# Slot tables from bf16 one-hot products, the slot table written before the weights' parts, and VectorE's order at the first expert

## The chip, the cores and the metric

The kernel runs on one core of a Trainium2 chip. The metric is the device time of one execution in microseconds (us), as the median of several executions. Matrix products run on TensorE (PE), elementwise work on VectorE (DVE) and ScalarE (ACT), gathers and some elementwise work on GpSimd (POOL), and SyncE (SP) issues most DMAs.

## The reference, cut to what matters

One decoder layer: a token mixer (not touched by the change), then a grouped top-2 mixture of 16 experts over 1024 tokens of width 1024.

```python
scores = jax.nn.sigmoid((hf @ w_router).astype(f32))
...                                    # best group of 4, top 2 experts in it: e_idx
w = jnp.take_along_axis(scores, e_idx, axis=-1)
w = w / jnp.sum(w, axis=-1, keepdims=True)
...
slot_tok = jnp.full((n_blk * MOE_BLOCK,), N, jnp.int32).at[dest].set((order // TOP_K).astype(jnp.int32))
slot_w = jnp.zeros((n_blk * MOE_BLOCK,), hf.dtype).at[dest].set(w.reshape(-1)[order].astype(hf.dtype))
...
a = jax.nn.silu(jnp.einsum('nrd,ndf->nrf', xs, w_gate[blk_e])) * jnp.einsum('nrd,ndf->nrf', xs, w_up[blk_e])
y = jnp.einsum('nrf,nfd->nrd', a, w_down[blk_e]).reshape(-1, D) * slot_w[:, None]
out = jnp.zeros((N + 1, D), hf.dtype).at[slot_tok].add(y)[:N]
```

Each (token, choice) pair has a slot in a list sorted by expert. `slot_tok` says which token sits in a slot and `slot_w` with what weight.

## The kernel before

**The stages.** The program runs adaLN rows and projections, then attention, the branch mix and output projection, the router, then routing tables and the experts. Each engine has its own program in order, and semaphores join them. The change lies between the router and the first expert's products, and everything behind it is the expert loop.

**The routing tables.** There are 1024 tokens in 8 tiles of 128, each with two choices, so 16 columns `a` (tile and choice) of 128 partitions. VectorE computes the slot of each pair (`dest`, L1471), splits it into position in the block (`pb_f[:, 0]`) and block number (`pb_f[:, 1]`), and builds one-hot tables: `hot_b` (L1477; 16 x 32 blocks), `hot_t` (L1480; `hot_b` times token number less position less 1024) and `hot_p` (L1483, in two halves of 8 columns; 16 x 128 positions). All are float32. Most of these instructions go through `own`, which makes VectorE wait for each result before the next one.

TensorE then adds up 16 products `hot_p[a]` x `hot_t[a]` in PSUM (L1900), which gives the token of each slot in [128 positions, 32 blocks], and 16 products `hot_p[a]` x `hot_b[a]` (L1904), where `hot_b` has by then been multiplied by the normalised weights (L1492). VectorE turns the first into `slot_idx` (L1495) and copies the second into `slot_w` (L1497).

**What follows.** GpSimd waits for `slot_ok` (L772), copies a column of `slot_idx` (L753) and gathers 128 rows of tokens into `xs` (L756). TensorE turns them (`expert_tokens`, L1911), ScalarE rounds them to a first part `xs_hi` (L998), VectorE makes the rest `xs_lo` (`expert_tokens_lo`, L1509). GpSimd issues the second block's gather and then subtracts the last sixth of the expert's weights (`expert_weights_rest`, L769).

**The weights of an expert** (gate, up, down, each [128, 4096] per partition) are split in the same way: ScalarE makes the first parts in six chunks of 2048 (L994), VectorE the rests of chunks 1 to 5 (`expert_weights_lo`, L1503), GpSimd the sixth. A product then takes three matmuls (L1921, L1922, L1926 for gate and up; L1964, L1965, L1969 for down).

**VectorE's order at the first expert** before: wait for `slot_w_full`, copy `slot_w`, five subtractions of L1503, `expert_tokens_lo(0)`, then, in its sequencer, `wait_ge(slot_w_ok)` and a `nop` that raises `a_ok` (L1526), then `expert_out(0)`. TensorE's first product waits for two things:

```python
pe.wait_ge(xs_lo_ok, j + 1)      # L1941
pe.wait_ge(a_ok, j * 2 + 1)      # L1942
```

Later it waits for the rests of the weights as it comes to them: `w_lo_ok` 1 and 2 in the gate's third pass, 3 and 4 in that of up, 5 and `w_lo_pool` in down.

Of the kernel before, what the change touches and what calls it, by code (L numbers as in the profile page):

```python
# [13 lines left out]
ALU = mybir.AluOpType  # L14
ACT = mybir.ActivationFunctionType
AX = mybir.AxisListType
F32 = mybir.dt.float32
F32R = mybir.dt.float32r
BF16 = mybir.dt.bfloat16
# [3 lines left out]
P = 128  # L23
BANK = 512
# [35 lines left out]
def hybrid_trunk(nc, x, c, w_ada, b_ada, g_norm_mix, g_norm_moe, w_in, cmp_pe_k, cmp_w1_k, cmp_w2_k, cmp_pe_v,  # L60
                 cmp_w1_v, cmp_w2_v, nsa_q_gain, nsa_k_gain, swa_q_gain, swa_k_gain, swa_sinks, w_branch_a,
                 w_branch_b, w_branch_c, w_out, w_router, router_bias, w_exp_gate, w_exp_up, w_exp_down, out):
    _, T, D = x.shape
    NT, NK = T // P, D // P
# [19 lines left out]
    with ctx:  # L84
        def sb(name, shape, dt=F32):
            return ctx.enter_context(nc.sbuf_tensor(name, shape, dt))
# [32 lines left out]
        bc, bc_r = twice("bc", [P, 8 * T])  # L119
# [5 lines left out]
        swa_bias = sb("swa_bias", [P, SWA_H, 2 * P])  # L125
# [13 lines left out]
        psum = ctx.enter_context(nc.psum_tensor("psum", [P, 8, BANK], F32))  # L139
# [76 lines left out]
        for i in ORDER:  # L216
            s = slot_of(i)
# [204 lines left out]
        def z_group(m):  # L422
# [20 lines left out]
        N_BLK = 2 * T // P + NE  # L443
# [18 lines left out]
        w12, dest_f = sb("w12", [P, 2, NT]), sb("dest_f", [P, 2, NT])  # L462
        dest = sb("dest", [P, 2, NT], U32)
        plan_f, plan_i = sb("plan_f", [P, 2 * NE + 2]), sb("plan_i", [P, 2 * NE + 2], I32)
        slot_idx, slot_w = sb("slot_idx", [P, N_BLK + 4], U32), sb("slot_w", [P, N_BLK + 4])
        in_idx, out_idx, w_cur = sb("in_idx", [P, 1], U32), sb("out_idx", [P, 1], U32), sb("w_cur", [P, 1])
        pb_u, pb_f = sb("pb_u", [P, 2, 2 * NT], U32), sb("pb_f", [P, 2, 2 * NT])
        tok_less, spare_row = sb("tok_less", [P, 2 * NT]), sb("spare_row", [P, 1])
        iota_p, iota_b = swa_bias[:, 0, 0:P], swa_bias[:, 1, 0:N_BLK]
        hot_p = bc[:, 6 * D:8 * D].rearrange("p (a s) -> p a s", a=2 * NT)  # L470
        hot_b, hot_t = (bc[:, 4 * D + i * BANK:4 * D + (i + 1) * BANK].rearrange("p (a b) -> p a b", a=2 * NT) for i in range(2))
        score_ok, chosen_ok, rank_full, dest_ok, routing_tables = (sem(s) for s in (
            "score_ok", "chosen_ok", "rank_full", "dest_ok", "routing_tables"))
        hot_ok, hot_w_ok, slot_full, slot_w_full, slot_ok, slot_w_ok = (sem(s) for s in (
            "hot_ok", "hot_w_ok", "slot_full", "slot_w_full", "slot_ok", "slot_w_ok"))
# [142 lines left out]
        def _(pool):  # L618
            one = Chain(pool, pool_own)
# [3 lines left out]
                                   pattern=[[-1, P]], channel_multiplier=1))  # L623
# [44 lines left out]
            for t, base, step, mult in ((tri_causal, 0, -1, 1), (tri_low, -1, 1, -1), (tri_strict, -1, -1, 1)):  # L668
# [3 lines left out]
                                       pattern=[[step, P]], channel_multiplier=mult))  # L672
            one(pool.memset(stair[:, :], 0.0))
            one(pool.affine_select(out=stair[:, :], in_=stair[:, :], compare_op=ALU.is_ge, fill=MASKED,
                                   base=16 * 56 - (CMP_LEN - 1), pattern=[[-CMP_STRIDE, 120]], channel_multiplier=1))

            one(pool.iota(swa_bias[:, 0, :], pattern=[[-1, 2 * P]], base=P, channel_multiplier=1,
                          allow_small_or_imprecise_dtypes=True))
# [8 lines left out]
            for k in (kwinT, kslcT):  # L687
# [3 lines left out]
                                       pattern=[[0, T]], channel_multiplier=1))  # L691
# [3 lines left out]
                                   pattern=[[1, T]], channel_multiplier=-SEL_BLOCK))  # L695
            one(pool.affine_select(out=blocks, in_=blocks, compare_op=ALU.is_ge, fill=0.0, base=SEL_BLOCK - 1,
                                   pattern=[[-1, T]], channel_multiplier=SEL_BLOCK))
            cend = kcmpT[ROW_POS:ROW_SEL, :]
            one(pool.iota(cend, pattern=[[CMP_STRIDE, NC + 1]], base=CMP_LEN - 1, channel_multiplier=0,
                          allow_small_or_imprecise_dtypes=True))  # L700
            one(pool.affine_select(out=cend, in_=cend, compare_op=ALU.is_equal, fill=0.0, base=0,
                                   pattern=[[0, NC + 1]], channel_multiplier=1))

            one(pool.iota(force[:, :, :], pattern=[[-2, NT], [1, NSEL]], base=0, channel_multiplier=0,
                          allow_small_or_imprecise_dtypes=True))
            pool.iota(stp[:, 30:31], pattern=[[0, 1]], base=0, channel_multiplier=1,
                      allow_small_or_imprecise_dtypes=True).then_inc(tables, 1)
# [10 lines left out]
            for m, r in enumerate(rides):  # L718
                w = width(r)
                pool.wait_ge(sb_z, m + 1)  # L720
                if m:
# [4 lines left out]
                          allow_small_or_imprecise_dtypes=True))  # L726
            one(pool.iota(iota_m[:, :], pattern=[[P, NT]], base=0, channel_multiplier=0,
                          allow_small_or_imprecise_dtypes=True))
            one(pool.iota(slot_idx[:, :], pattern=[[0, N_BLK + 4]], base=T, channel_multiplier=1))
            one(pool.memset(slot_w[:, :], 0.0))  # L730
            one(pool.iota(tok_less[:, :].rearrange("p (j n) -> p j n", j=2), pattern=[[0, 2], [P, NT]], base=-T,
                          channel_multiplier=1, allow_small_or_imprecise_dtypes=True))
            one(pool.iota(spare_row[:, :], pattern=[[0, 1]], base=T, channel_multiplier=1,
                          allow_small_or_imprecise_dtypes=True))
            pool.wait_ge(mix_done, 1)
# [5 lines left out]
                               pattern=[[1, P]], channel_multiplier=-1).then_inc(routing_tables, 1)  # L741
# [286 lines left out]
        def _(dve):  # L1028
            own = Chain(dve, dve_own)
# [83 lines left out]
            for s in range(4 * NT + 1):  # L1113
                ch, n = divmod(s, NT)
                a = psum[:, 4 + s % 3, :]
# [149 lines left out]
            for q, s in enumerate(slots):  # L1265
                n, i, u = s["n"], s["i"], s["unit"]
# [74 lines left out]
            for r in range(3 * 2 * NK):  # L1341
                m, b, hf = r // 6, r // 2 % 3, r % 2
# [112 lines left out]
            nb, base, last = plan_f[:, 0:NE], plan_f[:, NE:2 * NE], plan_f[:, 2 * NE:2 * NE + 1]  # L1455
# [12 lines left out]
            for j, oh in enumerate((oh1, oh2)):  # L1468
# [7 lines left out]
            own(dve.tensor_copy(pb_f[:, :, :], pb_u[:, :, :]))  # L1476
            own(dve.tensor_tensor(hot_b, iota_b.unsqueeze(1).to_broadcast([P, 2 * NT, N_BLK]),  # L1477
                                  pb_f[:, 1, :].unsqueeze(2).to_broadcast([P, 2 * NT, N_BLK]), ALU.is_equal))
            own(dve.tensor_tensor(tok_less[:, :], tok_less[:, :], pb_f[:, 0, :], ALU.subtract))
            own(dve.tensor_tensor(hot_t, hot_b, tok_less[:, :].unsqueeze(2).to_broadcast([P, 2 * NT, N_BLK]), ALU.mult))  # L1480
            for i in range(2):
                js = slice(i * NT, (i + 1) * NT)
                dve.tensor_tensor(hot_p[:, js, :], iota_p.unsqueeze(1).to_broadcast([P, NT, P]),  # L1483
# [1 line left out]
            for j, oh in enumerate((oh1, oh2)):  # L1485
                own(dve.tensor_tensor(t_a, score, oh, ALU.mult))
                own(dve.tensor_reduce(w12[:, j, :], t_a, AX.X, ALU.add))
            own(dve.tensor_tensor(red[1], w12[:, 0, :], w12[:, 1, :], ALU.add))
            own(dve.reciprocal(red[1], red[1]))
            for j in range(2):  # L1490
                own(dve.tensor_tensor(w12[:, j, :], w12[:, j, :], red[1], ALU.mult))
            dve.tensor_tensor(hot_b, hot_b, w12[:, :, :].rearrange("p j n -> p (j n)").unsqueeze(2).to_broadcast([P, 2 * NT, N_BLK]),  # L1492
                              ALU.mult).then_inc(hot_w_ok, 1)
            dve.wait_ge(slot_full, 1)
            dve.tensor_scalar(slot_idx[:, 2:N_BLK + 2], psum[:, 6, 0:N_BLK], spare_row[:, 0:1], None, ALU.add).then_inc(slot_ok, 1)  # L1495
            dve.wait_ge(slot_w_full, 1)
            dve.tensor_copy(slot_w[:, 2:N_BLK + 2], psum[:, 4, 0:N_BLK]).then_inc(slot_w_ok, 1)  # L1497

            def expert_weights_lo(e):
                for c in range(5):  # L1500
                    i, cs = c // 2, slice(c % 2 * SLOT // 2, (c % 2 + 1) * SLOT // 2)
                    dve.wait_ge(w_hi_ok, 6 * e + c + 1)
                    dve.tensor_tensor(ew_lo(e, i)[:, cs], w_raw(e, i)[:, cs], ew_hi[i][:, cs].bitcast(F32),  # L1503
                                      ALU.subtract).then_inc(w_lo_ok, 1)

            def expert_tokens_lo(j):
                for h in range(2):
                    dve.wait_ge(xs_hi_ok, j * 2 + h + 1)
                    ins = dve.tensor_tensor(xs_lo[:, 4 * h:4 * h + 4, :], psum[:, 2 + h, :].rearrange("p (k t) -> p k t", k=4),  # L1509
                                            xs_hi[:, 4 * h:4 * h + 4, :].bitcast(F32), ALU.subtract)  # L1510
                ins.then_inc(xs_lo_ok, 1)
# [6 lines left out]
                dve.scalar_tensor_tensor(y_sb.rearrange("p (a d) -> p a d", a=2), psum[:, 5:7, :], w_cur[:, 0:1],  # L1518
                                         gm_bc[:, :].rearrange("p (a d) -> p a d", a=2), ALU.mult, ALU.mult).then_inc(y_scaled, 1)

            expert_weights_lo(0)
            expert_tokens_lo(0)
            dve.wait_ge(dest_ok, 1)
            n_blk = dve.value_load(plan_i[0:1, 2 * NE:2 * NE + 1], min_val=NE, max_val=N_BLK - 1)
            dve.wait_ge(slot_w_ok, 1)
# [24 lines left out]
        def _(pe):  # L1550
# [59 lines left out]
            for s in range(4 * NT + 1):  # L1610
                ch, n = divmod(s, NT)
                if s < 4 * NT:
# [9 lines left out]
                    for k in range(NK):  # L1622
                        mm = pe.matmul(psum[:, 4 + s % 3, 0:w], hT[:, k, n * P:(n + 1) * P],  # L1623
                                       slot(slot_of(L_TOK + ch))[:, k, 0:w], start=(k == 0), stop=(k == NK - 1))
# [31 lines left out]
            for l in range(CMP_LEN):  # L1656
                w = slot(slot_of(L_W1 + l // 16), k=16)
                for a in range(2):
                    rs = slice(a * HD, (a + 1) * HD)
                    mm = pe.matmul(psum[0:NC, a, 0:CMP_HID], blk[rs, l, 0:NC], w[rs, l % 16, :],  # L1660
                                   start=(l == 0), stop=(l == CMP_LEN - 1))
# [10 lines left out]
            for hc in range(2):  # L1672
                pe.matmul(psum[0:64, 2, 0:HD], tmp_gk[:, hc, :], w2[:, 0, hc, :],
                          start=(hc == 0), stop=(hc == 1))
            for hc in range(2):
                mm = pe.matmul(psum[:, 3, 0:HD], tmp_gv[:, hc, :], w2[:, 1, hc, :], start=(hc == 0), stop=(hc == 1))
# [148 lines left out]
            for r in range(3 * 2 * NK):  # L1825
                m, b, hf = r // 6, r // 2 % 3, r % 2
# [14 lines left out]
                for k in range(k0, k1):  # L1841
                    mm = pe.matmul(bank, branch_lo(m)[:, k, :], o_hi[:, ns, k, :], start=False, stop=(k == k1 - 1))
# [9 lines left out]
            for i, m in enumerate((mod_a2, mod_b2)):  # L1852
                for k in range(NK):
                    mm = pe.matmul(psum[:, 4 + 2 * i + k // 4, (k % 4) * P:(k % 4 + 1) * P], m[:, k:k + 1].to_broadcast([P, P]),
                                   ident[:, :], start=True, stop=True)
            mm.then_inc(mod_rows, 1)
            pe.wait_ge(wr_in, 32)
            for n in range(NT + 2):
                if n < NT:
# [11 lines left out]
                    for h in range(2):  # L1871
                        w = wout_lo[h].rearrange("p (k n) -> p k n", k=NK)
                        for k in range(NK):
                            if n == 0 and k % 4 == 0:
                                pe.wait_ge(wout_lo_ok, 2 * h + k // 4 + 1)
                            mm = pe.matmul(psum[:, 2 * (n % 2) + h, :], y_hi[n % 2][:, k, :], w[:, k, :], start=False,
                                           stop=(k == NK - 1))
# [19 lines left out]
            for a in range(2 * NT):  # L1897
                if a % NT == 0:
                    pe.wait_ge(hot_ok, a // NT + 1)
                mm = pe.matmul(psum[:, 6, 0:N_BLK], hot_p[:, a, :], hot_t[:, a, :], start=(a == 0), stop=(a == 2 * NT - 1))  # L1900
            mm.then_inc(slot_full, 1)
            pe.wait_ge(hot_w_ok, 1)
            for a in range(2 * NT):
                mm = pe.matmul(psum[:, 4, 0:N_BLK], hot_p[:, a, :], hot_b[:, a, :], start=(a == 0), stop=(a == 2 * NT - 1))  # L1904
            mm.then_inc(slot_w_full, 1)


# [80 lines left out]
```

## Time and profile before

| | before |
|---|---|
| median of 3 runs | 2009.48 us (2003.45 to 2012.72) |
| the profiled execution's own time | 2009.4 us |
| its span, first to last instruction | 2007.7 us |
| mean granted TensorE clock | 0.947 |
| busy: PE, DVE, ACT, POOL | 91%, 46%, 33%, 18% |
| instructions | 22379 |

The span is 1.7 us less than that execution's own time. Busy shares are averages over all stages. The stage of this change lies in slice 31 of the page's 40, from 1505.8 to 1556.0 us, where PE is busy for three tenths only.

### The profile page before, as it was taken

To read this page: it belongs to the slowest core of one execution; us is meant where nothing else is said; L and a number is where in the kernel's file an instruction comes from. 1 tells how busy PE (TensorE), PEld (TensorE's weight loads), DVE (VectorE), ACT (ScalarE), POOL (GpSimd) and SP (SyncE) were. 2 spreads that over 40 slices of the span, in tenths; PEclk is the share of its full clock that TensorE was granted. 3 is DMA by queue.
4 is the path that set the end of the run, shared out by engine and by line. 5 is a ranking of instruction groups with operands and counts; after the bars stand their busy time and mean duration, and the time that the engine had idled before them with its cause. 6 is when DMAs were issued, how large, how long until landed. Compare 5 with 4: busy or idle time off the path is not lost. (4 is left out here: it accounts for less than half of the span.)

```text
span 2007.7 us, 22379 instructions
## 1 busy us (share of the span) xinstructions
PE 1817.4 (91%) x8125; PEld 1254.0 (62%) x8125; DVE 933.4 (46%) x1517; ACT 664.2 (33%) x1151; POOL 364.3 (18%) x315
## 2 busy tenths in 40 slices
PE   1999999989898989989989978899983999999996
PEld 1555654555555555655656656687873888888885
DVE  5554313232333342434333436477547464648475
ACT  1421101223232333423324325434212353537373
POOL 3211140000010100101102001100001243436344
PEclk9999998999999999999989988799995999999998
DMA  9334321201110010110000010174334586979694
GB/s 340 137 126 147 85 42 34 63 30 40 37 42 26 22 37 27 29 30 22 27 21 23 15 32 1 63 265 175 126 129 164 168 298 205 305 223 381 202 360 131
DMA packets 121395, 232.38 MB, mean 116 GB/s; under 512 B 5832, under 2 KB 44816, under 8 KB 120240
## 3 DMA queue, kind: packets, MB, share of 16 engines
q1 hardware_dynamic: 113312, 203.14, 29.0%
q0 software_dynamic: 7984, 27.93, 5.7%
q8 instruction: 61, 1.00, 0.2%
q14 instruction: 38, 0.31, 0.0%
HBM read 196.97 MB, written 35.13 MB: 116 GB/s over the span
## 5 line engine op out<-in xcount | busy, mean ns | idle before, releaser
L1797 PE MATMUL psum<-arena 128*128 128x512 f32 x768 | 386.7, 639 | 0.5 <-ACT arena L937 0.4
L1279 DVE TENSOR_REDUCE negm<-psum 128x1 f32<-128x640 f32 (+7 forms) x128 | 90.5, 707 | 423.2 <-PE psum L1724 423.2
L1783 PE MATMUL psum<-kv,arena 128*128 128x64 f32 x1464 | 201.6, 283 | 61.9 <-DVE arena L1255 36.7
L1783 PEld LDWEIGHTS psum<-kv,arena 128*128 128x128 f32 x1464 | 192.1, 204 | 69.6 <-issue 38.2
L723 POOL TENSOR_SCALAR arena<-arena 128x128 f32<-128x128 f32 (+7 forms) x32 | 76.8, 2401 | 854.9 <-ACT arena L931 854.9
L1797 PEld LDWEIGHTS psum<-arena 128*128 128x128 f32 x768 | 144.6, 204 | 128.0 <-issue 127.7
L908 ACT ACTIVATE arena<-psum,negm 128x640 f32<-128x640 f32 (+7 forms) x128 | 89.6, 700 | 402.1 <-DVE negm L1279 402.0
L1623 PE MATMUL psum<-arena 128*128 128x512 f32 (+2 forms) x512 | 189.0, 522 | 0.0
L1921 PE MATMUL psum<-heads_r,kv_r 128*128 128x512 f32 x384 | 150.7, 393 | 15.2 <-DVE kv_r L1509 15.2
L1722 PE MATMUL psum<-kv,heads 112*128 112x512 f32 (+7 forms) x384 | 150.7, 498 | 9.2 <-ACT arena L931 8.6
L1503 DVE TENSOR_TENSOR arena_r<-arena,heads_r 128x2048 fp32r<-128x2048 f32 x64 | 146.6, 2353 | 15.1 <-ACT heads_r L994 15.1
L1922 PE MATMUL psum<-heads_r,kv_r 128*128 128x512 f32 x384 | 150.5, 392 | 0.0
L1623 PEld LDWEIGHTS psum<-arena 128*128 128x128 f32 x512 | 95.9, 192 | 76.8 <-issue 73.9
L1751 PE MATMUL psum<-ident,arena 128*128 128x128 f32 x828 | 132.9, 283 | 9.8 <-ACT arena L390 6.1
L1722 PEld LDWEIGHTS psum<-kv,heads 112*128 112x128 f32 (+1 forms) x384 | 74.0, 204 | 95.2 <-issue 85.1
L769 POOL TENSOR_TENSOR arena_r<-arena,bc_r 128x2048 fp32r<-128x2048 f32 x16 | 102.8, 6427 | 107.1 <-ACT bc_r L994 107.0
L1751 PEld LDWEIGHTS psum<-ident,arena 128*128 128x128 f32 x828 | 94.0, 148 | 41.2 <-issue 27.7
L994 ACT ACTIVATE heads_r<-arena 128x2048 fp32r<-128x2048 f32 x64 | 117.3, 1914 | 0.9 <-DMA arena<-in_w_exp_up_dram 0.9
L1926 PE MATMUL psum<-arena_r,kv_r 128*128 128x512 f32 x384 | 95.0, 389 | 0.0
L1921 PEld LDWEIGHTS psum<-heads_r,kv_r 128*128 128x128 f32 x384 | 72.9, 190 | 30.8 <-issue 15.6
L1922 PEld LDWEIGHTS psum<-heads_r,kv_r 128*128 128x128 f32 x384 | 72.8, 190 | 15.2
L1926 PEld LDWEIGHTS psum<-arena_r,kv_r 128*128 128x128 f32 x384 | 72.1, 188 | 15.0
(376 smaller groups left out, 2729.1 us busy)
## 6 DMA issues: line engine op xcount, KB each, us to landing
arena<-in_w_exp_gate_dram SPq DMA_DIRECT2D x16, 2048.0 KB, 12.0
arena<-in_w_exp_down_dram SPq DMA_DIRECT2D x16, 2048.0 KB, 12.5
arena<-in_w_exp_up_dram SPq DMA_DIRECT2D x16, 2048.0 KB, 14.1
arena<-in_w_ada_dram SPq DMA_DIRECT2D x7, 2048.0 KB, 15.6
arena<-in_w_in_dram SPq DMA_DIRECT2D x24, 512.0 KB, 4.0
z_dram<-arena SPq DMA_DIRECT2D x48, 256.0 KB, 2.0
arena<-z_dram SPq DMA_DIRECT2D x8, 1536.0 KB, 7.9
bc<-in_w_ada_dram SPq DMA_DIRECT2D x4, 2048.0 KB, 7.8
```

Source lines behind the costliest of these rows:

```text
L769: pool.tensor_tensor(ew_lo(e, 2)[:, SLOT // 2:SLOT], w_raw(e, 2)[:, SLOT // 2:SLOT], ew_hi[2][:, SLOT // 2:SLOT].bitcast(F32), ALU.subtrac ...
L994: act.activation(ew_hi[i][:, cs], w_raw(e, i)[:, cs], ACT.Copy).then_inc(w_hi_ok, 1)
L1279: dve.tensor_reduce(m1, score_buf(u)[:, 0:w], AX.X, ALU.max, negate=True).then_inc(max_ok, 1)
L1503: dve.tensor_tensor(ew_lo(e, i)[:, cs], w_raw(e, i)[:, cs], ew_hi[i][:, cs].bitcast(F32), ALU.subtract).then_inc(w_lo_ok, 1)
L1623: mm = pe.matmul(psum[:, 4 + s % 3, 0:w], hT[:, k, n * P:(n + 1) * P], slot(slot_of(L_TOK + ch))[:, k, 0:w], start=(k == 0), stop=(k == NK ...
L1722: mm = pe.matmul(b[:, c0:c1], lhs, keys[:, k0 + c0:k0 + c1], start=True, stop=not masks)
L1751: ins = pe.transpose(bank[:, c * P:(c + 1) * P], src[:, t * P:(t + 1) * P], ident[:, :])
L1783: mm = pe.matmul(psum[:, bank, c * HD:(c + 1) * HD], pt[:, j * P:(j + 1) * P], v, start=(j == 0), stop=(j == u["nb"] - 1))
L1797: mm = pe.matmul(GATE_BANK, gate_w[t % 3][:, k, :], hT[:, k, hf * BANK:(hf + 1) * BANK], start=(k == 0), stop=(k == NK - 1))
L1921: pe.matmul(out, xs_hi[:, k, :], w_hi[:, k, :], start=(k == 0), stop=False)
L1922: pe.matmul(out, xs_lo[:, k, :], w_hi[:, k, :], start=False, stop=False)
L1926: mm = pe.matmul(out, xs_hi[:, k, :], w_lo[:, k, :], start=False, stop=(k == NK - 1))
```

## The change

The one-hot tables become bf16, and values that bf16 can't hold in one piece are split. The token of a slot is the sum of two products (`tile_row`, a multiple of 128, and `tok_rest`, partition less position), the weight the sum of three (`w_part`, three bf16 parts). The parts sit side by side in the columns of one matmul: 64 columns for the tokens, 96 for the weights. VectorE writes `slot_idx` before it computes the weights' parts. At the first expert it now does three subtractions of L1503, then `slot_w` (a reduction over the three parts in PSUM), then `expert_tokens_lo(0)`, then the other two subtractions.

```diff
+        hot_p = bc[:, 6 * D:7 * D].bitcast(BF16).rearrange("p (a s) -> p a s", a=2 * NT)
+        hot_b = bc[:, 4 * D:4 * D + 256].bitcast(BF16).rearrange("p (a b) -> p a b", a=2 * NT)
+        hot_t = bc[:, 4 * D + 256:4 * D + 768].bitcast(BF16).rearrange("p (a c b) -> p a c b", a=2 * NT, c=2)
+        hot_w = bc[:, 7 * D:7 * D + 768].bitcast(BF16).rearrange("p (a c b) -> p a c b", a=2 * NT, c=3)
...
-            one(pool.iota(tok_less[:, :].rearrange("p (j n) -> p j n", j=2), pattern=[[0, 2], [P, NT]], base=-T,
-                          channel_multiplier=1, allow_small_or_imprecise_dtypes=True))
+            one(pool.iota(tile_row[:, :].rearrange("p (j n) -> p j n", j=2), pattern=[[0, 2], [P, NT]], base=-T,
+                          channel_multiplier=0, allow_small_or_imprecise_dtypes=True))
+            one(pool.iota(tok_rest[:, :], pattern=[[0, 2 * NT]], base=0, channel_multiplier=1, allow_small_or_imprecise_dtypes=True))
...
-            own(dve.tensor_tensor(tok_less[:, :], tok_less[:, :], pb_f[:, 0, :], ALU.subtract))
-            own(dve.tensor_tensor(hot_t, hot_b, tok_less[:, :].unsqueeze(2).to_broadcast([P, 2 * NT, N_BLK]), ALU.mult))
+            own(dve.tensor_tensor(tok_rest[:, :], tok_rest[:, :], pb_f[:, 0, :], ALU.subtract))
+            for c, v in enumerate((tile_row, tok_rest)):
+                own(dve.tensor_tensor(hot_t[:, :, c, :], hot_b, v[:, :].unsqueeze(2).to_broadcast([P, 2 * NT, N_BLK]), ALU.mult))
...
+            dve.wait_ge(slot_full, 1)
+            own(dve.tensor_scalar(slot_part, psum[:, 6, 0:N_BLK], spare_row[:, 0:1], None, ALU.add))
+            dve.tensor_tensor(slot_idx[:, 2:N_BLK + 2], slot_part, psum[:, 6, N_BLK:2 * N_BLK], ALU.add).then_inc(slot_ok, 1)
             own(dve.tensor_tensor(red[1], w12[:, 0, :], w12[:, 1, :], ALU.add))
             own(dve.reciprocal(red[1], red[1]))
             for j in range(2):
                 own(dve.tensor_tensor(w12[:, j, :], w12[:, j, :], red[1], ALU.mult))
-            dve.tensor_tensor(hot_b, hot_b, w12[:, :, :].rearrange("p j n -> p (j n)").unsqueeze(2).to_broadcast([P, 2 * NT, N_BLK]),
-                              ALU.mult).then_inc(hot_w_ok, 1)
-            dve.wait_ge(slot_full, 1)
-            dve.tensor_scalar(slot_idx[:, 2:N_BLK + 2], psum[:, 6, 0:N_BLK], spare_row[:, 0:1], None, ALU.add).then_inc(slot_ok, 1)
-            dve.wait_ge(slot_w_full, 1)
-            dve.tensor_copy(slot_w[:, 2:N_BLK + 2], psum[:, 4, 0:N_BLK]).then_inc(slot_w_ok, 1)
-
-            def expert_weights_lo(e):
-                for c in range(5):
+            w16 = w12[:, :, :].rearrange("p j n -> p (j n)")
+            own(dve.tensor_copy(w_part[:, :, 0], w16))
+            own(dve.tensor_tensor(w_left[:, :], w16, w_part[:, :, 0], ALU.subtract))
+            own(dve.tensor_copy(w_part[:, :, 1], w_left[:, :]))
+            own(dve.tensor_tensor(w_left[:, :], w_left[:, :], w_part[:, :, 1], ALU.subtract))
+            own(dve.tensor_copy(w_part[:, :, 2], w_left[:, :]))
+            dve.tensor_tensor(hot_w, hot_b.unsqueeze(2).to_broadcast([P, 2 * NT, 3, N_BLK]),
+                              w_part[:, :, :].unsqueeze(3).to_broadcast([P, 2 * NT, 3, N_BLK]), ALU.mult).then_inc(hot_w_ok, 1)
+
+            def expert_weights_lo(e, chunks=range(5)):
+                for c in chunks:
...
-            expert_weights_lo(0)
+            expert_weights_lo(0, range(3))
+            dve.wait_ge(slot_w_full, 1)
+            dve.tensor_reduce(slot_w[:, 2:N_BLK + 2], psum[:, 4, 0:3 * N_BLK].rearrange("p (c b) -> p b c", c=3), AX.X,
+                              ALU.add).then_inc(slot_w_ok, 1)
             expert_tokens_lo(0)
+            expert_weights_lo(0, range(3, 5))
...
-                mm = pe.matmul(psum[:, 6, 0:N_BLK], hot_p[:, a, :], hot_t[:, a, :], start=(a == 0), stop=(a == 2 * NT - 1))
+                mm = pe.matmul(psum[:, 6, 0:2 * N_BLK], hot_p[:, a, :], hot_t[:, a, :, :].rearrange("p c b -> p (c b)"),
+                               start=(a == 0), stop=(a == 2 * NT - 1))
...
-                mm = pe.matmul(psum[:, 4, 0:N_BLK], hot_p[:, a, :], hot_b[:, a, :], start=(a == 0), stop=(a == 2 * NT - 1))
+                mm = pe.matmul(psum[:, 4, 0:3 * N_BLK], hot_p[:, a, :], hot_w[:, a, :, :].rearrange("p c b -> p (c b)"),
+                               start=(a == 0), stop=(a == 2 * NT - 1))
```

## Rows read from the trace of the kernel before

**Rows 1.** Windows: busy us of each engine (instructions), granted PE clock, DMA share, GB/s.

```profile
1522.90:1529.70 6.80, 6.79 (x32) 6.79 (x33) 3.55 (x10) 0.00 (x0) 0.00 (x0) 0.50 0.18 73
...
1538.60:1553.70 15.10, 0.00 (x0) 0.00 (x0) 15.06 (x9) 2.35 (x3) 8.44 (x3) 0.50 0.12 35
1553.70:1557.90 4.20, 4.14 (x10) 3.30 (x11) 1.19 (x1) 0.00 (x0) 1.84 (x2) 0.50 0.00 0
...
1800.00:1900.00 100.00, 99.54 (x467) 81.42 (x467) 67.97 (x67) 56.58 (x53) 48.59 (x26) 1.00 0.89 303
```

**Rows 2.** Waits from 1553.7 us to the end: engine, releaser, total us, times, longest.

```profile
PE psum L1921 <- DVE kv_r L1509: 15.2, 1, 15.2
```

**Rows 3.** Chain that ended last, 1536 to 1554 us: start, us, what.

```profile
1540.63 0.02 DVEq L1526
...
1543.53 8.78 DVE arena_r L1503 x2
1552.31 1.21 DVE kv_r L1509 x2
...
1553.76 0.76 PE psum L1921
```

**Rows 4.** Timeline from the one-hot tables on: start, us, engine, line [idle before].

```profile
1519.98 0.69 DVE L1477 TENSOR_TENSOR bc<-swa_bias,pb_f 128x512 f32<-128x512 f32 x1
...
1521.64 2.36 DVE L1483 TENSOR_TENSOR bc<-swa_bias,pb_f 128x1024 f32<-128x1024 f32 x2
...
1522.91 7.04 PE L1900 MATMUL psum<-bc 128*128 128x32 f32 x32 [10.25 <-DVE bc L1483]
...
1525.20 0.17 DVE L1488 TENSOR_TENSOR kv<-w 128x8 f32<-128x8 f32 x1
...
1526.04 0.69 DVE L1492 TENSOR_TENSOR bc<-bc,w 128x512 f32<-128x512 f32 x1
...
1529.77 7.01 PE L1904 MATMUL psum<-bc 128*128 128x32 f32 x32
1529.99 0.25 DVE L1495 TENSOR_SCALAR slot_idx<-psum,spare_row 128x32 uint32<-128x32 f32 x1 [3.27 <-PE psum L1900]
...
1536.59 1.95 PE L1911 MATMUL psum<-ident,kv 128*128 128x128 f32 x8
1536.82 0.19 DVE L1497 COPY slot_w<-psum 128x32 f32<-128x32 f32 x1 [6.57 <-PE psum L1904]
...
1538.58 1.08 ACT L998 ACTIVATE kv_r<-psum 128x512 fp32r<-128x512 f32 x2 [22.30 <-PE psum L1911]
```

**Rows 5.** Timeline, DVE, 1547 to 1549 us.

```profile
1543.53 6.58 DVE L1503 TENSOR_TENSOR arena_r<-arena,heads_r 128x2048 fp32r<-128x2048 f32 x1
```

**Rows 6.** Timeline, POOL, the first two gathers and its share of the weights.

```profile
1531.50 1.12 POOL L756 DMA_INDIRECT kv<-xn_dram,in_idx  x1 [0.89 <-POOL in_idx L753]
1538.69 0.56 POOL L753 COPY in_idx<-slot_idx 128x1 uint32<-128x1 uint32 x1 [6.07 <-PE psum L1911]
1540.05 2.21 POOL L756 DMA_INDIRECT kv<-xn_dram,in_idx  x1 [0.81 <-POOL in_idx L753]
1542.30 5.67 POOL L769 TENSOR_TENSOR arena_r<-arena,bc_r 128x2048 fp32r<-128x2048 f32 x1
```

**Rows 7.** Timeline at the second expert, DVE, then POOL.

```profile
1598.55 2.29 DVE L1503 TENSOR_TENSOR arena_r<-arena,bc_r 128x2048 fp32r<-128x2048 f32 x1
...
1600.94 1.28 DVE L1518 SCALAR_TENSOR_TENSOR bc<-psum,w_cur,gm_bc 128x1024 f32<-128x1024 f32 x1
...
1598.81 6.49 POOL L769 TENSOR_TENSOR arena_r<-arena,bc_r 128x2048 fp32r<-128x2048 f32 x1 [9.87 <-ACT bc_r L994]
```

**Rows 8.** Instructions of the bf16 product at L1895.

```profile
L1895 PEld LDWEIGHTS psum<-chosen,before_b x1: 106/106/106, 1512.3 to 1512.3; 128*128 128x128 bf16 x1
L1895 PE MATMUL psum<-chosen,before_b x1: 266/266/266, 1512.3 to 1512.3; 128*128 128x128 bf16 x1
```

**Rows 9.** Gathers into `kv`, first two, issue to landing.

```profile
DMA to landing us min/median/max: 4.3/4.9/5.5
```

More of the change, by code:

```diff
@@ L467, in hybrid_trunk @@
         pb_u, pb_f = sb("pb_u", [P, 2, 2 * NT], U32), sb("pb_f", [P, 2, 2 * NT])
-        tok_less, spare_row = sb("tok_less", [P, 2 * NT]), sb("spare_row", [P, 1])
+        tile_row, tok_rest, spare_row = sb("tile_row", [P, 2 * NT]), sb("tok_rest", [P, 2 * NT]), sb("spare_row", [P, 1])
+        w_part, w_left = sb("w_part", [P, 2 * NT, 3], BF16), sb("w_left", [P, 2 * NT])
         iota_p, iota_b = swa_bias[:, 0, 0:P], swa_bias[:, 1, 0:N_BLK]
-        hot_p = bc[:, 6 * D:8 * D].rearrange("p (a s) -> p a s", a=2 * NT)
-        hot_b, hot_t = (bc[:, 4 * D + i * BANK:4 * D + (i + 1) * BANK].rearrange("p (a b) -> p a b", a=2 * NT) for i in range(2))
+        slot_part = swa_bias[:, 2, 0:N_BLK]
+        hot_p = bc[:, 6 * D:7 * D].bitcast(BF16).rearrange("p (a s) -> p a s", a=2 * NT)
+        hot_b = bc[:, 4 * D:4 * D + 256].bitcast(BF16).rearrange("p (a b) -> p a b", a=2 * NT)
+        hot_t = bc[:, 4 * D + 256:4 * D + 768].bitcast(BF16).rearrange("p (a c b) -> p a c b", a=2 * NT, c=2)
+        hot_w = bc[:, 7 * D:7 * D + 768].bitcast(BF16).rearrange("p (a c b) -> p a c b", a=2 * NT, c=3)
         score_ok, chosen_ok, rank_full, dest_ok, routing_tables = (sem(s) for s in (
```

## The prediction

> **What bounds the kernel now.** I read the windows first. In the expert loop, shown from 1800 to 1900 us, PE is busy for over 99% of the time at the full clock, and in the stretch of the change it stands still: 15.1 us without one product [rows 1]. The waits from the first expert's product to the end hold one row of PE as a waiting engine, the 15.2 us in front of that product [rows 2]. So what is won ahead of it should reach the end one for one: the next experts' weights, gathers and adds all wait for events of the loop and move with it. The question is when L1921 starts, now at 1553.76.
>
> The chain of waits [rows 3] and the timeline [rows 4] tell how that time comes about. One-hot tables until 1524.00; 16 products for the token table, 7.04 us; 16 for the weights, 7.01 us; the rows turned and `slot_w` copied until 1537.01. Then VectorE alone: five subtractions, then `expert_tokens_lo`, which runs from 1552.31 to 1553.52, and PE starts 0.24 later. Between 1537.01 and 1552.31 lie 15.30 us for five instructions. The last of the five follows the fourth after its 6.58 us and ends in 8.78 us with it, so one takes 2.20, five take 11.0, and 4.3 are a stall of the fourth [rows 3, 5].
>
> The stall is GpSimd's. Its own subtraction runs from 1542.30 to 1547.97, and the VectorE instruction that starts at 1543.53 ends 2.1 us behind that, about its normal length [rows 5, 6]. At the second expert the order is reversed: VectorE's subtraction ends at 1600.84, and GpSimd's, begun at 1598.81, ends at 1605.30, 4.46 us later [rows 7]. The two engines take turns on such instructions. But L1518, which reads PSUM and SBUF, runs at 1600.94 in its plain 1.28 us under that same GpSimd instruction [rows 7].
>
> **Tables and token products.** The second `hot_t` product costs VectorE one more 512-element instruction, 0.69 plus 0.04 of hand-over: 0.73 (two of these and a small one took 1521.64 - 1519.98 = 1.66 [rows 4]). `hot_p` ends at 1524.00 + 0.73 = 1524.73. The output type alone should not change VectorE's pace here, as inputs stay float32. The first eight products hide behind the second half of `hot_p`; the other eight follow it. A bf16 load of 128x128 takes 0.106 us and the product behind it 0.266, most of it latency [rows 8]. Overlapped they cost some 0.11 each, so 0.9 plus 0.3 for the last: slot_full at 1526.0, where it was 1529.99 [rows 4]. Bounds: not overlapped at all, 8 x 0.37 = 3.0, so 1527.8; if the loads cost half, 1525.6. I take 0.11, since in the float32 products, too, the pitch is near one load (7.04 / 32 = 0.22).
>
> VectorE reaches that wait at 1525.20 + 0.73 = 1525.93, so it is hardly early. Two instructions like L1495 (0.25 each, 0.04 between) write `slot_idx` at 1526.54, where it was 1530.24: 3.7 us earlier [rows 4].
>
> **Weights' parts.** Normalising takes 1526.04 - 1525.20 = 0.84, four instructions of 0.21. Five more such small ones: 1.05. `hot_w` has 1536 elements: between 1.18 for 1024 and 2.29 for 2048, so 1.73 [rows 4, 7]. VectorE is free at 1526.54 + 0.84 + 1.05 + 1.73 = 1530.16. Bound above: a four-dimensional pattern at half pace, 3.4; below: two elements at a time, the time of 768, between 0.69 for 512 and 1.18 for 1024, 0.94. The Trainium skill (VectorE: DVE Perf Modes, Mode 2×_1P) has 16-bit operands in steps of one run at two per cycle; `w_part` is broadcast with step 0, so by that rule too it would be the slow way. Were it the quick one, PE would start 0.8 us earlier still. No row here has such an instruction.
>
> **The weight products leave the path.** They run from 1530.2: 16 x 0.11 + 0.2 is 2.0 us, to 1532.2 (5.9 if not overlapped: 1536.1), while VectorE already subtracts. Their cover is 6.6 us of subtractions, up to 1536.8.
>
> **Gather.** From the end of L1495 to the gather's issue are 1531.50 - 1530.24 = 1.26 us, and 4.3 to its landing [rows 4, 6, 9]: 1526.54 + 5.56 = 1532.1. PE then turns the rows from 1532.2, ScalarE comes 2.0 us behind its start (1538.58 against 1536.59) and takes 1.08: `xs_hi` is done by 1535.4 [rows 4]. If PE's unoverlapped end of 1536.1 held, this would be 1539.2.
>
> **The reordered piece.** Three subtractions, 6.6: 1536.8. The reduction of `slot_w`, a PSUM read of 96 elements, 0.3 (L1495 took 0.25 for 32): 1537.1. `expert_tokens_lo` 1.21: 1538.3. PE 0.24 later: 1538.55. That is 15.2 us sooner than 1553.76. By terms: VectorE's first subtraction starts at 1530.16, not 1537.01 (6.85); two subtractions go behind (4.4); the stall goes behind (4.3); the reduction replaces nothing in that span (-0.3); sum 15.2.
>
> **Where the stall goes.** GpSimd's second gather starts when the rows are turned, near 1534.5, and its subtraction came 3.6 us after that (1542.30 - 1538.69 [rows 6]): 1538.1, or up to 2.3 later. That is behind the third subtraction in any case, and `expert_tokens_lo` reads PSUM, like L1518, so the stall falls on the fourth or fifth: VectorE ends them at 1538.3 + 4.4 + 4.4 = 1547.1. PE needs the fourth's result only at its 44th product (24 of gate, 16 of up's first passes, 4 of the third); at the loop's full-clock mean of 99.54 / 467 = 0.21 us [rows 1] that is at least 9.4 us in, 1547.9, and the fourth is done by 1544.9 even with the whole stall on it. The fifth comes after 48 products and the transposes, over 10.2 us in, 1548.8 or later, against 1547.1. The cover is 3 and 1.7 us at the least. What is late next is VectorE itself: `xs_lo` waits for its three subtractions, not for the rows.
>
> **The condition on it.** PE also waits for `a_ok`, and the `nop` that raises it stands behind all five subtractions. Before, the same `nop` went out at 1540.63, while the second of five was being computed: VectorE's sequencer runs ahead of its engine, with the rest queued [rows 3]. It needs `slot_w_ok` (1537.1 now), so it should fire near 1537.2, ahead of `xs_lo`.
>
> **Rivals.**
> *A. The sequencer does not run ahead, so PE waits for all five subtractions.* Then 1547.1 + 0.3 = 1547.4, a gain of 6.4: 2003.0 us. Against it stands the row at 1540.63; for it, that the queue now also holds the reduction. 8 in 100.
> *B. GpSimd's turn comes before the third subtraction.* It would add 4.4: a gain of 10.8, 1998.6 us. For that its second gather would have to be through by 1534.6, when it has only just begun. 6 in 100.
> *C. The first gather is held up by VectorE,* which was idle at 1530 to 1537 and is now busy. The copy of 0.56 and the issue of 2.21 us, against 1.12 for the first, show what that costs when long subtractions run: 1.5 us [rows 6]; twice a whole instruction would be 4.5. The rows then come at 1536.6, `xs_hi` at 1539.9, `xs_lo` 0.6 later; PE near 1540.8: a gain of 13, 1996.4 us. 8 in 100. The Trainium skill (GPSIMD Engine Reference, Key points) says that GpSimd contends with VectorE instructions that have two SBUF inputs, which `hot_w` and the subtractions are; by that, the gather's index copy could wait for one of them. The rows agree in kind.
> *D, the other side: the low clock holds on.* PE was busy for 6.79 of 6.80 us with the float32 table products, and its clock stayed at 0.50, 1.2 GHz; the loop's first 4.2 us, ten products, ran at 0.50 too, and those from 1800 on at 1.00 [rows 1]. Each further us at half clock costs about half a us: a clock that stays low for 30 us more eats the gain, for 50 us more makes it slower by 0.5%. The loop's products are the same as before and follow each other as before, so 3 in 100. A start a few us earlier or later against the clock's rise is worth 1 to 2 us either way.
> *E. Something outside cancels it,* such as a loop that is held by weight transfers (DMA share 0.89 between 1800 and 1900 [rows 1]), so that less than 5 us arrives: 5 in 100. Against it: PE is busy 99.54 of 100 us there, and the transfers are started by PE's own steps.
>
> **How the numbers follow.** The likeliest, at 70 in 100: 15.2 us off the profiled execution's 2009.4 (span 2007.7 plus 1.7 around it; the median of the three runs is 2009.48, the same): 1994.2 us. Its own range is 1989 to 1999: the three runs differ by 9 us, so their median may be off by 3; bounds of `hot_w` (+0.8, -1.7), products (+0.4, -1.8), clock (2). Eight in ten over all cases: 1988.5 to 2003, which takes in A, B and C. Within 0.5%, 10 us, is about what a measurement of this kernel can't tell from no change. Faster by more (below 1999.4): nearly all of the likeliest (0.66), C (0.07) and half of B (0.03), so 0.76. Within: the rest of these, A, E, so 0.21. Slower: 0.03 from D.
>
> **What would show it.** L1921 first starts at 1538 to 1539; before it VectorE shows three subtractions of 2.28 without a gap from about 1530, a reduction, two L1509s; the nop near 1537. The instruction of 6.6 us is the fourth or fifth subtraction, behind PE's start. L1904 takes some 2 us and hides. If L1921 still follows the fifth subtraction, A holds; if one of the first three is 6.6 long, B. The prediction is wrong if PE then waits in the first block for `w_lo_ok`, or if the loop's length from L1921 to the end is no longer 454 us.

## The result, and the profile after

| | before | after |
|---|---|---|
| median | 2004.98 us (2003.45 to 2012.72, 5 runs) | 1991.39 us (1989.98 to 1996.44, 5 runs) |
| ratio, 95% interval | 1 | 0.9930 (0.9913 to 0.9946) |
| profiled execution, span | 2009.4, 2007.7 us | 1993.5, 1991.7 us |

The kernel is faster by 0.7%, 14 us at the ratio. Forecast were 1994.2 us and 15.2 us of gain. The next fences show how the 16.0 us between the two spans come about.

The chain of waits of the changed kernel from 1534 us on; L1514 is the weights' subtraction (L1503 before), L1520 `expert_tokens_lo`, L1938 the first expert product (L1921 before); "DVEq" is VectorE's sequencer, and it answers to [rows 3]:

```profile
1536.43 0.22 DVEq L1539
...
1537.00 0.25 DVE slot_w L1534
...
1537.39 0.32 DVEq L1544
...
1537.93 0.53 DVE kv_r L1520
1538.46 0.24 issue
1538.70 0.77 PE psum L1938
```

The first product starts at 1538.70 where it was 1553.76, 0.24 us behind `xs_lo`. At 1536.43 the sequencer is at L1539, code that stands behind all five subtractions, while the third is being computed (until 1537.09). It has gone ahead, as at 1540.63 before, and passes the `nop` (L1541, an event semaphore in the trace) at 1537.3, ahead of the end of `xs_lo`:

```profile
L1541 DVEq EVENT_SEMAPHORE  x1: 21/21/21, 1537.3 to 1537.3; - x1
```

The timeline of VectorE (L1482 is `hot_b`, L1486 the two `hot_t`, L1489 `hot_p`), against [rows 4, 5]:

```profile
1520.48 0.69 DVE L1482 TENSOR_TENSOR bc<-swa_bias,pb_f 128x512 bf16<-128x512 f32 x1
...
1522.14 0.69 DVE L1486 TENSOR_TENSOR bc<-bc,tok_rest 128x512 bf16<-128x512 bf16 x1
1522.87 2.36 DVE L1489 TENSOR_TENSOR bc<-swa_bias,pb_f 128x1024 bf16<-128x1024 f32 x2
...
1526.43 0.25 DVE L1495 TENSOR_SCALAR swa_bias<-psum,spare_row 128x32 f32<-128x32 f32 x1
1526.72 0.19 DVE L1496 TENSOR_TENSOR slot_idx<-swa_bias,psum 128x32 uint32<-128x32 f32 x1
...
1528.72 1.76 DVE L1507 TENSOR_TENSOR bc<-bc,w_part 128x1536 bf16<-128x1536 bf16 x1
1530.40 6.69 DVE L1514 TENSOR_TENSOR arena_r<-arena,heads_r 128x2048 fp32r<-128x2048 f32 x3
1537.00 0.25 DVE L1534 TENSOR_REDUCE slot_w<-psum 128x32 f32<-128x96 f32 x1
1537.17 1.28 DVE L1520 TENSOR_TENSOR kv_r<-psum,kv_r 128x512 fp32r<-128x512 f32 x2
1538.37 2.28 DVE L1514 TENSOR_TENSOR arena_r<-arena,heads_r 128x2048 fp32r<-128x2048 f32 x1
1540.57 6.68 DVE L1514 TENSOR_TENSOR arena_r<-arena,bc_r 128x2048 fp32r<-128x2048 f32 x1
```

From `hot_b` to the first product are now 1538.70 - 1520.48 = 18.22 us, where they were 1553.76 - 1519.98 = 33.78: 15.56 less. This stage length is the measure in all that follows. The instruction with the stall, 6.68 us, is the fifth subtraction, and it starts 1.9 us behind PE.

PE's timeline of the table products (L1915 tokens, L1920 weights) and of the rows' turning:

```profile
1524.15 0.61 PE L1915 MATMUL psum<-bc 128*128 128x64 bf16 x8 [10.98 <-DVE bc L1489]
1525.29 0.61 PE L1915 MATMUL psum<-bc 128*128 128x64 bf16 x8 [0.53 <-DVE bc L1489]
1530.54 1.46 PE L1920 MATMUL psum<-bc 128*128 128x96 bf16 x16 [4.64 <-DVE bc L1507]
1532.71 1.97 PE L1928 MATMUL psum<-ident,kv 128*128 128x128 f32 x8 [0.71 <-DMA kv<-xn_dram,in_idx]
```

14 us of float32 products have become 2.7. The weights' products end at 1532.0, inside the first subtraction, and PE then waits 0.71 for the gather.

GpSimd's timeline, against [rows 6] (L758 the index copy, L761 the gather, L774 its subtraction):

```profile
1528.16 1.12 POOL L761 DMA_INDIRECT kv<-xn_dram,in_idx  x1 [0.89 <-POOL in_idx L758]
1534.82 2.31 POOL L758 COPY in_idx<-slot_idx 128x1 uint32<-128x1 uint32 x1 [5.55 <-PE psum L1928]
1537.94 0.99 POOL L761 DMA_INDIRECT kv<-xn_dram,in_idx  x1 [0.81 <-POOL in_idx L758]
1538.95 6.15 POOL L774 TENSOR_TENSOR arena_r<-arena,bc_r 128x2048 fp32r<-128x2048 f32 x1
```

The first gather's issue took 1.12 us, as before. It began while VectorE had only short instructions. `hot_w`, which has two inputs in SBUF, began 0.56 us later, at 1528.72, and didn't lengthen it. In the same way the second issue took 0.99 us, though a subtraction began 0.43 us into it. The second index copy ends at 1537.13, right behind VectorE's third subtraction (1537.09).

Windows of the first products, against [rows 1]:

```profile
1538.70:1541.60 2.90, 2.90 (x7) 2.32 (x8) 2.90 (x2) 0.00 (x0) 2.87 (x2) 0.51 0.55 174
1541.70:1545.00 3.30, 3.30 (x16) 2.71 (x15) 3.30 (x1) 0.00 (x0) 3.30 (x1) 1.00 0.02 9
```

PE's clock reached 2.4 GHz after seven products and 2.9 us, not after ten and some 4.2. From the first product to the end of the span are 453.0 us, 0.9 less than the 453.9 before; in the eleven profiles of this document that length lies between 452.6 and 454.5, so the 0.9 can't be put down to the change. Together: stage -15.6, loop -0.9, and `hot_b` itself started 0.5 later, so -16.0.

### The profile page after: what moved, and what is told of

It is laid out like the page before. It is cut to its first block and busy times, and to the rows that moved or that the text cites. A ratio compares the mean times of both kernels' runs of the same rounds, so it can differ in the third digit from the quotient of the medians.

```text
span 1991.7 us, 22324 instructions
## 1 busy us (share of the span) xinstructions
PE 1805.6 (91%) x8093; PEld 1241.9 (62%) x8093; DVE 936.9 (47%) x1524; ACT 664.2 (33%) x1151; POOL 365.6 (18%) x316
## 5 line engine op out<-in xcount | busy, mean ns | idle before, releaser
L1938 PE MATMUL psum<-heads_r,kv_r 128*128 128x512 f32 x384 | 150.3, 391 | 4.0 <-DVE kv_r L1520 4.0
L1514 DVE TENSOR_TENSOR arena_r<-arena,heads_r 128x2048 fp32r<-128x2048 f32 x64 | 142.5, 2286 | 15.1 <-ACT heads_r L999 15.1
L774 POOL TENSOR_TENSOR arena_r<-arena,bc_r 128x2048 fp32r<-128x2048 f32 x16 | 103.4, 6464 | 106.9 <-ACT bc_r L999 106.9
L1938 PEld LDWEIGHTS psum<-heads_r,kv_r 128*128 128x128 f32 x384 | 72.6, 189 | 19.5 <-issue 4.4
```

The lines of the kernel that those rows point to most:

```text
L774: pool.tensor_tensor(ew_lo(e, 2)[:, SLOT // 2:SLOT], w_raw(e, 2)[:, SLOT // 2:SLOT], ew_hi[2][:, SLOT // 2:SLOT].bitcast(F32), ALU.subtrac ...
L1938: pe.matmul(out, xs_hi[:, k, :], w_hi[:, k, :], start=(k == 0), stop=False)
```

## The experiments

Each kernel was timed beside the kernel before. "Stage" is the time from `hot_b` to the first expert product in its profile.

| kernel | stage us | less than before | ratio to the kernel before (95%) |
|---|---|---|---|
| before | 33.78 | | 1 |
| after | 18.22 | 15.6 | 0.9930 (0.9913 to 0.9946) |
| after again | 18.21 | 15.6 | 0.9929 (0.9916 to 0.9941) |
| old order, new tables | 28.56 | 5.2 | 0.9971 (0.9958 to 0.9985) |
| new order, old tables | 23.15 | 10.6 | 0.9952 (0.9934 to 0.9969) |
| `a_ok` held | 26.46 | 7.3 | 0.9959 (0.9945 to 0.9973) |
| before, no GpSimd share | 29.48 | 4.3 | 0.9976 (0.9958 to 0.9993) |
| `slot_idx` late | 22.81 | 11.0 | 0.9962 (0.9949 to 0.9975) |
| new order, old tables, after the copy | 21.50 | 12.3 | 0.9940 (0.9921 to 0.9959) |
| two first | 16.28 | 17.5 | 0.9913 (0.9899 to 0.9927) |
| two first, `slot_idx` sooner | 16.22 | 17.6 | 0.9927 (0.9913 to 0.9942) |

**The tables with the old order.** The edit to the changed kernel:

```diff
-            expert_weights_lo(0, range(3))
             dve.wait_ge(slot_w_full, 1)
             dve.tensor_reduce(slot_w[:, 2:N_BLK + 2], ...).then_inc(slot_w_ok, 1)
+            expert_weights_lo(0)
             expert_tokens_lo(0)
-            expert_weights_lo(0, range(3, 5))
```

> The changed kernel with VectorE's old order at the first expert (wait for the weight products, write slot_w, five subtractions, then xs_lo). Measured as the time from the start of hot_b to the first expert product: 33.8 us before, 18.2 us after. My theory, order and tables both count: the subtractions start when the bf16 weight products are through, some 2 us later than after, and two subtractions (4.4) and GpSimd's turn (4.3) come back in front of PE: 28.6 us, about 5 us under the kernel before. Rival, the tables bring the gain and the order is free: near 20 us and 13 us under the kernel before. Rival, the tables bring nothing: 33 us.

The stage took 28.56 us. VectorE's timeline in it:

```profile
1527.54 0.26 DVE L1533 TENSOR_REDUCE slot_w<-psum 128x32 f32<-128x96 f32 x1 [1.56 <-PE psum L1919]
1527.71 8.89 DVE L1514 TENSOR_TENSOR arena_r<-arena,heads_r 128x2048 fp32r<-128x2048 f32 x4
1536.52 6.58 DVE L1514 TENSOR_TENSOR arena_r<-arena,bc_r 128x2048 fp32r<-128x2048 f32 x1
1543.03 1.28 DVE L1520 TENSOR_TENSOR kv_r<-psum,kv_r 128x512 fp32r<-128x512 f32 x2
```

VectorE waits 1.56 us for the weights' products, and the 6.58 us stall is back ahead of `xs_lo`. The tables alone bring 5.2 us. With them in place, the order is worth the other 10.3.

**The order with the old tables.** The edit to the kernel before:

```diff
-            dve.wait_ge(slot_w_full, 1)
-            dve.tensor_copy(slot_w[:, 2:N_BLK + 2], psum[:, 4, 0:N_BLK]).then_inc(slot_w_ok, 1)
...
-            expert_weights_lo(0)
+            expert_weights_lo(0, range(3))
+            dve.wait_ge(slot_w_full, 1)
+            dve.tensor_copy(slot_w[:, 2:N_BLK + 2], psum[:, 4, 0:N_BLK]).then_inc(slot_w_ok, 1)
             expert_tokens_lo(0)
+            expert_weights_lo(0, range(3, 5))
```

> The kernel before, float32 tables, with only the new order (three subtractions, slot_w, xs_lo, two subtractions). My theory: VectorE is free at once after slot_idx, so its three subtractions hide the float32 weight products, and what is late is the gather, whose index copy now meets a subtraction and waits some 2 us for it. Rows near 1538, turned, split: 22.1 us from hot_b to the first product, 11 to 12 us under the kernel before. Rival, the two engines don't meet on so small a copy: 20 to 21 us, PE bound by its own float32 products. Rival, the order is worth only the two subtractions and the stall behind it (8.7): 25 us.

It took 23.15 us, 1.0 more than my number, and the timelines of GpSimd and of PE say where:

```profile
1524.81 2.07 POOL L753 COPY in_idx<-slot_idx 128x1 uint32<-128x1 uint32 x1 [35.29 <-DVE slot_idx L1495]
1527.77 2.25 POOL L756 DMA_INDIRECT kv<-xn_dram,in_idx  x1 [0.89 <-POOL in_idx L753]
```

```profile
1524.16 7.01 PE L1905 MATMUL psum<-bc 128*128 128x32 f32 x32
1533.35 1.97 PE L1912 MATMUL psum<-ident,kv 128*128 128x128 f32 x8 [2.18 <-DMA kv<-xn_dram,in_idx]
```

I had counted one meeting, that is, one wait of GpSimd for a VectorE subtraction to end. There were two: the index copy took 2.07 us instead of 0.18, and the issue 2.25 instead of 1.12. PE was through with its float32 products and waited 2.18 us for the rows. So the order alone gives 10.6 of the 15.6 us, and the bf16 tables add 4.9 on top.

**Is it a meeting?** The same kernel with one line ahead of the first subtraction:

```diff
+            dve.wait_ge(in_idx_ok, 1)
             expert_weights_lo(0, range(3))
```

> The kernel with float32 tables and the new order alone (23.1 us from hot_b to the first product), and one wait more: VectorE begins its first subtraction only when GpSimd has copied the gather's index. In the run without that wait the index copy took 2.07 us and the gather's issue 2.25, against 0.18 and 1.12 in the kernel before. My theory: each of the two meets one subtraction. With the wait the copy takes 0.18 again, the issue still meets a subtraction and stays near 2.2, the rows land 1.9 us sooner, and PE starts at 21.2 us, although VectorE starts 0.4 later. Rival: the copy is slow for another reason, such as GpSimd waking from a long wait: copy and 23.1 stay, or become 23.5. Rival: the bound is PE's float32 products: 22 to 23.

```profile
1523.67 0.18 POOL L753 COPY in_idx<-slot_idx 128x1 uint32<-128x1 uint32 x1 [35.28 <-DVE slot_idx L1495]
1524.75 2.42 POOL L756 DMA_INDIRECT kv<-xn_dram,in_idx  x1 [0.89 <-POOL in_idx L753]
```

The copy is back to 0.18, the issue, which no wait protects, took 2.42, and the stage is 1.65 us shorter (21.50, where 21.2 was expected), though VectorE waited 0.40 us for the copy. The rows came 0.5 us behind the last float32 product, so the rival with PE as the bound is out as well. The Trainium skill (GPSIMD Engine Reference, Key points) names two SBUF inputs on VectorE as what contends with GpSimd. The copy agrees with it, and so does L1518 of [rows 7], which reads PSUM and ran at its plain length beside GpSimd's subtraction. The runs show the turns and their lengths, not what the two engines share.

**`slot_idx` late.** In the changed kernel the three lines from `wait_ge(slot_full, 1)` to `slot_ok` were moved behind `hot_w`.

> The changed kernel with slot_idx written behind hot_w, as the kernel before did. slot_idx comes 3.7 us later, straight ahead of the first subtraction. My theory: GpSimd's index copy then meets that subtraction and waits for it (2.1 us), so that the rows land at 1538.0 and PE starts 21.6 us after hot_b, 3.4 later than after the change. Without that meeting the rows land at 1536 and PE starts at 19.7. If the place of slot_idx doesn't matter because VectorE is the bound: 18.2.

```profile
1528.69 2.07 POOL L758 COPY in_idx<-slot_idx 128x1 uint32<-128x1 uint32 x1 [35.01 <-DVE slot_idx L1508]
1531.65 2.25 POOL L761 DMA_INDIRECT kv<-xn_dram,in_idx  x1 [0.89 <-POOL in_idx L758]
```

It took 22.81 us, 4.6 more than after and 1.2 more than expected, for the same reason: copy 2.07 and issue 2.25, two meetings. PE stood 7.51 us in front of the rows. The rows' turning began 18.6 us behind `hot_b`, not 12.2: 3.6 come from the later write and 3.0 from the two meetings (1.9 and 1.1), 0.2 more than the 6.4 together, and 4.6 reached PE. That is what the move of `slot_idx` in the change is worth with the rest in place. The timing agrees only loosely here (0.9962, 7.6 us, where the stage says 11.0; the interval reaches to 10.2).

**What the running ahead is worth.** In the changed kernel, before the `nop` that raises `a_ok`:

```diff
             dve.wait_ge(slot_w_ok, 1)
+            dve.wait_ge(w_lo_ok, 5)
             dve.nop().then_inc(a_ok, 1)
```

> The changed kernel, where VectorE's sequencer waits for all five subtractions before the nop that raises a_ok. It shows what rival A would have cost. PE's first product then follows the fifth subtraction: 27.0 us from hot_b instead of 18.2, 8.8 us slower than the changed kernel. If the sequencer's running ahead were not what let PE go, nothing would change: 18.2.

```profile
1544.47 0.80 PE L1939 MATMUL psum<-heads_r,kv_r 128*128 128x512 f32 x1 [12.34 <-DVEq L1542]
```

PE waited 12.34 us, now for the sequencer. The stage took 26.46 us, 8.2 more than after and 0.5 less than expected. Had the sequencer not gone ahead, more than half of the gain would have been lost.

**Whose stall it was.** In the kernel before, GpSimd's subtraction was left out at the first expert and VectorE did it behind `expert_tokens_lo`:

```diff
-                expert_weights_rest(e)
+                if e:
+                    expert_weights_rest(e)
...
             expert_tokens_lo(0)
+            dve.wait_ge(w_hi_ok, 6)
+            dve.tensor_tensor(ew_lo(0, 2)[:, SLOT // 2:SLOT], w_raw(0, 2)[:, SLOT // 2:SLOT], ew_hi[2][:, SLOT // 2:SLOT].bitcast(F32),
+                              ALU.subtract).then_inc(w_lo_pool, 1)
```

> The kernel before, with GpSimd's subtraction left out at the first expert and done by VectorE behind xs_lo. If the 4.3 us in the fourth subtraction are GpSimd's turn, all five take 2.28 and the first product comes 4.3 us sooner: 29.5 us from hot_b instead of 33.8. If they are something else on VectorE (a weight transfer, code loading), a subtraction of 6.6 us stays and so does 33.8.

```profile
1535.02 8.89 DVE L1504 TENSOR_TENSOR arena_r<-arena,heads_r 128x2048 fp32r<-128x2048 f32 x4
1543.82 2.28 DVE L1504 TENSOR_TENSOR arena_r<-arena,bc_r 128x2048 fp32r<-128x2048 f32 x1
```

All five subtractions now have their plain length, and the stage is 4.3 us shorter. The 4.3 us were GpSimd's turn.

**A better split.** After the change the rows were split by 1535.8 us while VectorE's third subtraction ran until 1537.1. So two ahead of `slot_w` and `xs_lo`, three behind; the changed kernel ran once more with it.

> The changed kernel once more, as the mate of the next three on one chip: 18.2 us from hot_b to the first product, 0.993 of the kernel before.

```diff
-            expert_weights_lo(0, range(3))
+            expert_weights_lo(0, range(2))
...
-            expert_weights_lo(0, range(3, 5))
+            expert_weights_lo(0, range(2, 5))
```

> The changed kernel with two subtractions ahead of slot_w and xs_lo instead of three. After the change the rows are split by ScalarE at 1535.8 while VectorE is busy with its third subtraction until 1537.0. My theory: with two, PE starts when the gather's path ends, 16.3 us from hot_b instead of 18.2, and the three late subtractions with GpSimd's turn still lie under PE's first products: about 2 us faster than the changed kernel, no wait of PE for w_lo_ok. Rival: the third one, or GpSimd's turn in front of it, comes too late for PE, which then waits in up's third pass: no gain. Rival: the path is VectorE's in another way and 18.2 stays.

The chain of waits in it:

```profile
1529.44 0.61 ACT kv_r L1003
...
1530.07 0.69 DVE kv_r L1520
...
1531.49 0.03 DVEq L1541
1531.53 0.08 issue
1531.61 0.77 PE psum L1938
```

The stage took 16.28 us, 1.9 less than after, and the chain now comes from ScalarE's split of the rows. PE never waited for `w_lo_ok`. The profile names the `nop` at 1531.49 as its release, 0.13 us behind the end of `xs_lo`, since the sequencer comes to that code only when it has passed the wait for `xs_hi`. But PE starts 0.25 us behind `xs_lo`, where the kernel before has 0.24, so the `nop` delays nothing that can be measured; whether it would bind on a still shorter path is not shown. The medians of that session were 1987.88 us for this kernel and 1991.62 for the changed one. Each of its four runs was faster than each of the five of the changed kernel, but the two intervals in the table overlap, so the gain over the change is shown by the stage and only made likely by the times.

**And `slot_idx` sooner.** As the last one, with the wait for `slot_full` and the two instructions behind it placed after the first half (`j == 0`) of the loop at L1491 of the changed kernel.

> As the one before, and slot_idx written after the first half of the gathering of the weights, not after both. After the change slot_full came at 1525.9, but VectorE took it up at 1526.4. If the gather's path bounds the start, this moves it by another 0.5 us: 15.8 us from hot_b. If not, 16.3 as in the one before.

A miss: 16.22 us, not 15.8. `slot_idx` was 0.4 us sooner, but `expert_tokens_lo` no longer waited for ScalarE. It followed the reduction, at 1530.17, 14.7 us behind `hot_b` as before, because VectorE had the same work ahead of it and now waited 0.25 us for `slot_full`. The bound had gone back to VectorE. The times say 14.6 us for this kernel where the stage says 17.6, and the interval (11.6 to 17.5) just misses it; its six runs fall between 1987.5 and 1995.1 us.

## Why the prediction was right

Numbers are us behind `hot_b`, forecast (from 1519.98) and measured (from 1520.48).

- **Tables.** `hot_p` done at 4.75, measured 4.75. One more `hot_t` instruction was its whole price.
- **Token products.** slot_full at 6.0, measured 5.4. The term was mis-sized: eight products took 0.61 us with the last, not 1.2. It changed little, since VectorE came to that wait at 5.95, as forecast. `slot_idx` was ready at 6.43 against 6.56: 0.07 from the wait, 0.06 from its second instruction, which took 0.19 and not 0.25. The ground for 0.11 us a product was also misread: the float32 pitch of 0.22 is not near one load, whose record is 0.33 us:

```profile
L1900 PEld LDWEIGHTS psum<-bc x32: 288/333/338, 1522.9 to 1529.5; 128*128 128x128 f32 x32
```

- **Weights' parts.** 10.18, measured 10.00. `hot_w` took 1.76 us (forecast 1.73), so it kept the pace of the float32 rows, though both inputs are bf16. The rule of the Trainium skill for 16-bit operands (VectorE: DVE Perf Modes, Mode 2×_1P) asks for steps of one, and the step of 0 fits with the slow pace.
- **Gather.** Rows in at 12.1, measured 12.2. Rival C didn't come about: copy and issue of the first gather began among short instructions. The experiments show that it was a real danger: with a subtraction right behind `slot_idx` the rows come some 3 us later by two meetings, between the 1.5 and the 4.5 of the prediction.
- **Reordered piece.** First product at 18.57, measured 18.22.
- **The stall** went behind PE's start, on the fifth subtraction, and nobody waited for it. Rival B fails with it.
- **The condition on `a_ok`** held (rival A, measured at 26.46 us of stage, a gain of 7.3 where I had put 6.4).
- **The clock** rose sooner, not later (rival D), and the loop passed on all of the gain (rival E): from the first product to the end 453.0 us against 453.9, as good as the same.

The forecast of 15.2 us stood against 15.6 in the stage and 15.9 between the profiled executions. The median of five runs before is 4.5 us below that of the three I had, which is why the gain of the medians is 13.6 with a time that is 2.8 below my 1994.2. So the closeness of that time to the forecast says little either way, as spread moved its base by more; the stage is what bears the sum out. The 4.4 us of two subtractions and the 4.3 of the stall are borne out together by `a_ok` held, which gives back 8.2 of these 8.7, and the 4.3 alone by the kernel without GpSimd's share. The 6.85 us that VectorE starts sooner were put down in one sum. The order alone already brings them: its first subtraction starts 10.2 us behind `hot_b` with the old tables, 9.9 with the new ones and 17.0 before. What the tables save with the new order is the wait for the rows. The parts are worth 5.2 (tables) and 10.6 (order) alone, 15.8 together, against 15.6 measured. That they nearly add up is a coincidence of two different bounds: with the copy's meeting gone the order alone gives 12.3.

## What to carry to other kernels

When a chain is held by one engine that does bulk work in front of a small result, ask of each bulk instruction when its own reader comes. Here two of five, and another engine's turn on the shared resource, lay in front of a product that needed none of them for 9 us. Write an index that GpSimd waits for while VectorE has short instructions ahead, not in front of a long one with two SBUF inputs, since both the copy and the gather's issue may have to wait one out when it is under way as they begin. After moving work, look at what ends last in the new chain: in two further attempts it was ScalarE's rows and then VectorE again, with stages of 16.28 and 16.22 us.

## What the runs showed of the hardware

- Eight bf16 products of 64 columns at half clock (1.2 GHz) took 0.61 us with the last one's 0.24, so one each (0.61 - 0.24) / 7 = 0.053 us, while each weight load of 128x128 shows 0.102 to 0.132 us in the rows below. Sixteen of 96 columns took 1.46 us with 0.28 for the last, 0.079 each. So the pace went with the columns, and the recorded length of a load was not the bound on it that I had taken it for.

```profile
L1915 PEld LDWEIGHTS psum<-bc x16: 102/132/132, 1524.1 to 1525.6; 128*128 128x128 bf16 x16
L1915 PE MATMUL psum<-bc x16: 233/242/242, 1524.2 to 1525.7; 128*128 128x64 bf16 x16
```

- GpSimd's subtraction of 2048 columns takes 4.5 us when no VectorE subtraction is under way as it begins (4.51 with `a_ok` held, 4.56 with two first), and 5.66 to 6.49 when it begins inside one [rows 6, 7]. Its spans include the wait. The wait goes both ways: a VectorE subtraction that began under it took 6.27 us with `a_ok` held, not 2.28.
- A gather's issue took 2.21 to 2.42 us when a VectorE subtraction was under way as it began, and 0.99 to 1.12 when none was, also where `hot_w` or a subtraction began 0.43 us or more into it.
- Much of the spread between runs arises before the change's stage. In the eleven profiles `hot_b` starts between 1513.2 and 1520.5 us, with nothing changed ahead of it but the small tables that GpSimd fills. The windows from 250 to 1480 us show a granted clock of 0.95 for the five in which it starts at 1513.2 to 1516.0, and 0.94 for the six at 1517.5 to 1520.5. The stage itself repeated within 0.01 us (18.22 and 18.21), so a stage length from one profile can tell apart what the times of five runs don't. What makes the clock lower in some executions stays open.
